# Two-layer diffusion backbone on one core: three of layer 1's modulation products moved to layer 0's router and to the gap between the layers

## The reference, cut to what matters

```python
mod = silu(c) @ w_mod[l] + b_mod[l]          # one row of 6 * 1024 for each group
shift1, scale1, gate1, shift2, scale2, gate2 = split(mod, 6)
y = token_mixing(x * (1 + scale1) + shift1, ...)
x = layer_norm(ALPHA * x + gate1 * y, ...)
y = hier_moe(x * (1 + scale2) + shift2, ...)
x = layer_norm(ALPHA * x + gate2 * y, ...)
```

## Time and profile before

| | us |
|---|---|
| timed executions | 1424.7, 1426.8, 1427.19 |
| median | 1426.8 |
| profiled execution, its own time | 1428.1 |
| profiled execution, span from first to last instruction | 1426.3 |
| layer 1: input projection to router | about 730 to 1155 |
| layer 0: router to first expert | about 445 to 482 |

### The profile page before, as it was taken

The page is one execution under the profiler, slowest core; times in us unless marked ns, Lnnn a source line. Parts: engine busy times, 40 slices in busy tenths (PEclk is TensorE's granted clock), DMA queues, the critical chain, the costliest instruction groups (busy, mean ns, idle before and its releaser), DMA issues. The chain is left out here.

```text
span 1426.3 us, 17205 instructions
## 1 busy us (share of the span) xinstructions
PE 1360.6 (95%) x6802; PEld 745.1 (52%) x6802; DVE 509.1 (36%) x975; ACT 222.4 (16%) x429; POOL 148.8 (10%) x130
## 2 busy tenths in 40 slices
PE   5999999999999999999989999999999999999994
PEld 2665545445445655555537655544554465555552
DVE  1224454432134422322352345452413343232324
ACT  0021220222201111111110213122230111011110
POOL 0002431022100000000001034302120000000000
PEclk9999999999999999999999999999999999999998
DMA  9755545556457399999964635544436729999993
GB/s 380 259 209 196 213 191 181 210 198 244 197 198 315 138 392 370 414 412 413 393 260 157 243 139 182 195 170 189 175 139 265 295 76 395 404 390 396 412 411 138
DMA packets 44345, 376.31 MB, mean 264 GB/s; under 512 B 13050, under 2 KB 17274, under 8 KB 21628
## 3 DMA queue, kind: packets, MB, share of 16 engines
q1 hardware_dynamic: 35856, 372.18, 65.1%
q10 hardware_dynamic: 8428, 3.29, 0.9%
HBM read 371.11 MB, written 4.33 MB: 263 GB/s over the span
## 5 line engine op out<-in xcount | busy, mean ns | idle before, releaser
L943 PE MATMUL psum<-ring,hT 128*128 128x512 f32 x960 | 432.0, 598 | 5.1 <-DVE hT L1398 2.5
L943 PEld LDWEIGHTS psum<-ring,hT 128*128 128x128 f32 x960 | 177.3, 191 | 206.1 <-issue 198.4
L1049 PE MATMUL psum<-ring,tbuf 128*64 128x256 f32 x1920 | 216.0, 380 | 3.6 <-DMA ring<-in_stream 3.6
L1049 PEld LDWEIGHTS psum<-ring,tbuf 128*64 128x64 f32 x1920 | 135.9, 137 | 97.1 <-issue 17.8
L1088 PE MATMUL psum<-ring,tbuf 128*64 128x512 f32 x512 | 116.9, 598 | 3.1 <-ACT tbuf L1332 1.9
L1755 DVE TENSOR_SCALAR tbuf<-tbuf 128x256 f32<-128x256 f32 x32 | 9.4, 295 | 244.5 <-ACT tbuf L1322 244.5
L1609 DVE TENSOR_TENSOR ch<-psum,bias_ring 128x512 f32<-128x512 f32 x56 | 38.7, 691 | 140.3 <-PE psum L943 140.3
L939 PE MATMUL psum<-hT,ring 128*128 128x256 f32 x384 | 85.4, 380 | 0.0
L967 PE MATMUL psum<-ring,tbuf 128*128 128x512 f32 x192 | 82.9, 593 | 0.0
L939 PEld LDWEIGHTS psum<-hT,ring 128*128 128x128 f32 x384 | 72.5, 190 | 13.0 <-issue 3.7
L1913 POOL TENSOR_SCALAR ldata<-ldata 128x512 f32<-128x512 f32 x24 | 46.1, 1922 | 257.3 <-ACT ldata L1284 245.6
(11 more groups left out here) (270 smaller groups left out, 1172.5 us busy)
## 6 DMA issues: line engine op xcount, KB each, us to landing
ring<-in_stream SPq DMA_DIRECT2D x158, 2048.0 KB, 9.7
ch<-in_stream SPq DMA_DIRECT2D x6, 2048.0 KB, 13.0
bias_ring<-in_b_in SPq DMA_DIRECT2D x30, 256.0 KB, 8.0
ldata<-in_ldata SPq DMA_DIRECT2D x2, 2329.0 KB, 19.8
hbuf<-in_ln SPq DMA_DIRECT2D x4, 1024.0 KB, 12.4
hbuf<-in_stream SPq DMA_DIRECT2D x1, 2048.0 KB, 8.7
tbuf<-in_stream SPq DMA_DIRECT2D x1, 2048.0 KB, 11.9
hbuf<-row_mem SPq DMA_DIRECT2D x2, 1024.0 KB, 4.7
```

Of the source, the lines that this page charges most:

```text
L943: mm = pe.matmul(bank(PJ + g), hT[:, k, g * P:(g + 1) * P], w[:, k, :], start=(k == 0), stop=(k == KT - 1))
L1049: mm = pe.matmul(psum[halves_of[hf], UP[j], 0:FE // 2], xgT[:, k, halves_of[i]], w_up[:, k, hf * (FE // 2):(hf + 1) * (FE // 2)], start=(k ...
```

## The change

Layer 1 keeps five modulation slots in its own projection, 7 to 11, after chunks 2, 5, 8, 11 and 14. Slots 4 and 5 are multiplied at layer 0's router in place of `hold_clock` products, both into bank 5, which DVE adds once. Slot 6 is multiplied between the layers into bank 1; ACT copies the bank to `sig`, and POOL adds that to `rows`. Slot 4 is loaded to `tbuf`, slot 5 in two halves to parts of `ch` and `hbuf`, slot 6 to the first `ahead_slot`. Because half of slot 5 lies where the constants of the second normalisation go, SP waits for the two router products ahead of `norm_and_gates`. The `hold_clock` products that remain at the router go to other PSUM areas.

```diff
-              dict(zip([2, 4, 6, 8, 10, 12, 14, 16], [(1, m) for m in range(4, N_MOD)]))]
+              dict(zip([2, 5, 8, 11, 14], [(1, m) for m in range(7, N_MOD)]))]
+ROUTER_MODS, LAYER_MODS = [4, 5], [6]
...
+        mod_half = [chf[:, 0:SLOT // 2], hbuf[:, 0:SLOT // 2]]
...
                 for j in range(AHEAD):
                     sp.dma_start(ahead_slot[j], dram["stream"][l * SLOTS + FIRST_EXPERT_SLOT + j]).then_inc(ahead_loaded[j], 16)
+                if l + 1 < DEPTH:
+                    sp.dma_start(early_slot[1], dram["stream"][stream_slot("mod", l + 1, ROUTER_MODS[0])]).then_inc(router_mod_loaded[0], 16)
                 sp.wait_ge(yt_ready, l * 4 + 4)
+                if l + 1 < DEPTH:
+                    for i in range(2):
+                        sp.dma_start(mod_half[i], dram["stream"][stream_slot("mod", l + 1, ROUTER_MODS[1]), :, i * (SLOT // 2):(i + 1) * (SLOT // 2)])\
+                          .then_inc(router_mod_loaded[1], 16)
+                    sp.wait_ge(router_mods_filled, 1)
                 norm_and_gates(l, 1)
...
                 first_pass()
+                if l + 1 < DEPTH:
+                    for j, m in enumerate(LAYER_MODS):
+                        sp.dma_start(ahead_slot[j], dram["stream"][stream_slot("mod", l + 1, m)]).then_inc(layer_mods_loaded[j], 16)
...
+                def router_mod(m, w, start, stop):
+                    for k in range(KT):
+                        j = k % 4
+                        mm = pe.matmul(psum[MROWS * j:MROWS * (j + 1), 5, :], scZ[:, k, ZC - 2 * m:ZC - 2 * m + MROWS], w[k],
+                                       start=(start and k < 4), stop=(stop and k >= 4))
+                    return mm
...
                         x_turned(l, 0, g)
+                        if g == 1:
+                            pe.wait_ge(layer_mods_copied, 1)
...
                 tokens_back(0)
-                hold_clock(3)
+                if l + 1 < DEPTH:
+                    hold_clock(1)
+                    pe.wait_ge(router_mod_loaded[0], 16)
+                    w = early_slot[1].rearrange("p (k n) -> p k n", k=KT)
+                    router_mod(ROUTER_MODS[0], [w[:, k, :] for k in range(KT)], True, False)
+                else:
+                    hold_clock(3)
                 turn_x(l, 1, 1, 6)
-                hold_clock(2)
+                hold_clock(4, psum[:, 4, W // 2:W])
...
                 tokens_back(1)
-                hold_clock(5)
+                if l + 1 < DEPTH:
+                    pe.wait_ge(router_mod_loaded[1], 32)
+                    w = [half_.rearrange("p (k n) -> p k n", k=KT // 2) for half_ in mod_half]
+                    router_mod(ROUTER_MODS[1], [w[k // 4][:, k % 4, :] for k in range(KT)], False, True).then_inc(router_mods_filled, 1)
+                    hold_clock(3, bank(7))
+                else:
+                    hold_clock(5, bank(7))
...
                 if l + 1 < DEPTH:
-                    hold_clock(3)
+                    for j, m in enumerate(LAYER_MODS):
+                        pe.wait_ge(layer_mods_loaded[j], 16)
+                        mm = mod_products(ahead_slot[j].rearrange("p (k n) -> p k n", k=KT), m, 1, True, True)
+                    mm.then_inc(layer_mods_filled, 1)
+                    hold_clock(2)
...
                         modulate(l + 1, 0, g, 2 + 2 * g)
+                        if g == 0:
+                            act.wait_ge(layer_mods_filled, 1)
+                            act.activation(sig, bank(1), ACT.Copy).then_inc(layer_mods_copied, 1)
...
+                if l + 1 < DEPTH:
+                    dve.wait_ge(router_mods_filled, 1)
+                    dve.wait_ge(rows_added, MOD_ADDS.index((1, ROUTER_MODS)))
+                    tt(rows[:, l + 1, :], rows[:, l + 1, :], bank(5), ALU.add).then_inc(rows_added, 1)
                 dve.wait_ge(ranked, l + 1)
...
+                if l + 1 < DEPTH:
+                    pool.wait_ge(layer_mods_copied, 1)
+                    pool.wait_ge(rows_added, MOD_ADDS.index((1, LAYER_MODS)))
+                    tt(rows[:, l + 1, :], rows[:, l + 1, :], sig, ALU.add).then_inc(rows_added, 1)
```

More of the change, by code:

```diff
@@ L77 @@
 MODS_AFTER = [dict(zip([2, 3, 5, 6, 7, 9, 10, 11, 13, 14, 15, 16], [(0, m) for m in range(4, N_MOD)] + [(1, m) for m in range(4)])),
-              dict(zip([2, 4, 6, 8, 10, 12, 14, 16], [(1, m) for m in range(4, N_MOD)]))]
-MOD_ADDS = [(0, m) for m in EARLY_MOD] + [(l, [m]) for after in MODS_AFTER for l, m in after.values()]
+              dict(zip([2, 5, 8, 11, 14], [(1, m) for m in range(7, N_MOD)]))]
+ROUTER_MODS, LAYER_MODS = [4, 5], [6]
+MOD_ADDS = [(0, m) for m in EARLY_MOD] + [(l, [m]) for l, m in MODS_AFTER[0].values()] \
+    + [(1, ROUTER_MODS), (1, LAYER_MODS)] + [(l, [m]) for l, m in MODS_AFTER[1].values()]
 MROWS = 32
@@ L409, in build @@
         mod_ready = sem("mod_ready")
+        router_mod_loaded = [sem(f"router_mod_loaded{i}") for i in range(len(ROUTER_MODS))]
+        router_mods_filled = sem("router_mods_filled")
+        layer_mods_loaded = [sem(f"layer_mods_loaded{i}") for i in range(len(LAYER_MODS))]
+        layer_mods_filled, layer_mods_copied = sem("layer_mods_filled"), sem("layer_mods_copied")
         rows_summed = sem("rows_summed")
@@ L496, in all_added @@
         def all_added(l):
-            return 2 + sum(len(after) for after in MODS_AFTER[:l + 1])
+            return 2 + len(MODS_AFTER[0]) if l == 0 else len(MOD_ADDS)
         def used(l, i):
@@ L892, in turn_branch, with hold_clock @@
                     mm.then_inc(br_turned, 1)
-                def hold_clock(n):
+                def router_mod(m, w, start, stop):
[4 more added lines that the diff above has]
+                    return mm
+                def hold_clock(n, out_=bank(5)):
                     for _ in range(n):
-                        pe.matmul(bank(5), ident, const[:, 0:W], start=True, stop=True)
+                        pe.matmul(out_, ident, const[:, 0:out_.shape[-1]], start=True, stop=True)
                 def before_first_chunk(q):
@@ L1282, in _ @@
                         act.wait_ge(proj_read, proj(l, c, g))
+                        if (l, c, g) == (1, 12, 0):
+                            act.wait_ge(rows_added, MOD_ADDS.index((1, LAYER_MODS)) + 1)
                         v = ch[:, g, GATE_BUF[c - 12], :]
```

## The result

The changed kernel takes 1418.2 us (median of four runs, 1416.7 to 1420.7), the kernel before 1426.05 beside it: ratio 0.9947, 95% interval 0.9932 to 0.9963, 7.9 us less.

A forecast was written before the change was run, and what follows sets the result against it. PE's own queue was taken to bound the kernel (busy 95% of the span). Projections -5.6, router +0.14 and gap +0.2 gave -5.2 us, from the median 1426.8 to 1421.6 us; range 1419.5 to 1425.2.

The forecast's parts named there:

- 3 x 1.86: Layer 1's projections: net three products leave PE's queue, each holding PE for 1.86 us, 5.6 us in all.
- Later expert slots are issued when PE frees a buffer, as before: Layer 0's experts: loads after the first slots keep their issue rule; no gain or cost was counted.
- Projections: Layer 1's projections: five products out, two in, 5.6 us less; bounds 5.9 with pauses, 1.9 if two products give nothing.
- Rival 1: Layer 1's projections: the time comes back as waits behind chunks 10 and 12, leaving -1.6 us, 1425.2; chance 0.14.
- Router: Layer 0's router: the second product with its fillers takes 4.44 instead of 4.30 us, costing 0.14, up to 0.3.
- The first product is covered: Layer 0's router: slot 4's product ends at 457.94, before DVE's normalised `x` at 458.01, so it costs nothing.
- Loads behind SP's wait: Layer 0's first expert slots land near 478.6, 483.5 and 488.4, margins 3.9, 2.5 and 3.0 us: no cost.
- rivals 2 and 3: Layer 0's first expert loads late: by up to 0.6 us (1422.2 us, chance 0.08), or 9.2 us (1432.3 us, chance 0.05).
- Gap: Between the layers: group 0's turn comes about 1.0 us later, layer 1's first chunk about 0.2; bounds 0 and 1.0.
- ACT's cover: Between the layers: ACT's part of the modulation had 0.8 us to spare before the first chunk, all used up.
- rival 4: Layer 0's router: the change doesn't do what it says, a clock that falls there; near 1427 us, chance 0.03.
- the range's low end: Whole kernel: 5.9 us gained and no costs, 1420.9, less 1.4 for the spread of the runs: 1419.5 us.

The follow-up runs named there:

- e4: The changed kernel unaltered, run again beside the kernel before for more runs and a second profile: 1420.4 us (seven runs, ratio 0.9962).

## Why the prediction missed, point by point

Two steps failed. "3 x 1.86" was too small a price for three products, by some 0.4 us. "Later expert slots are issued when PE frees a buffer, as before" took PE's waits for those slots as a constant; that, as far as the profiles tell, is most of the rest and what put the time outside the range. Another 0.75 us of the distance to the forecast is its base: the kernel before stood at 1426.8 us when the forecast was made and at 1426.05 beside the changed one.

- **Projections: right in kind, 0.45 us short.** Forecast 5.6, bound 5.9; measured 6.06, and 6.02 as the mean of four profiles each. The step that failed is "3 x 1.86". The 1.86 runs from the product's start to that of the work behind it. PE's starts, matched between the two profiles, show two more pieces. Behind chunk 10 the projection ahead of the product starts at 933.40 and the round behind it at 938.78, 5.38 us apart; without the product it is 932.13 and 935.57, 3.44. So 1.94 goes, 0.1 of it ahead of the product. The round behind then takes 1.78 us instead of 1.89 to the next projection, another 0.1:

```profile
933.40 3.60 PE L943 MATMUL psum<-ring,hT 128*128 128x512 f32 x8
```

  In this way each of the five products taken out wins 2.01 to 2.05 us, and each of the two put in costs 2.05. The prediction had the piece ahead, as 0.1 a product, in the bound and not in the sum; it had nothing for the piece behind. Rival 1 is out: no round came late, and PE's waits are still 1.2 and 0.6 us, as in the earlier trace rows (790 to 1110 us):

```profile
PE psum L878 <- issue: 1.2, 1, 1.2
...
PE psum L878 <- ACTq L1294: 0.6, 1, 0.6
```

- **Router: 0.33 against 0.14**, 0.25 net of the 0.08 won behind it. The first product is covered, as said: PE turns `x` at 459.13, 1.06 later than before, and all was 1.07 late. The four narrow fillers take what the two wide ones took (460.06 to 461.97, against 458.99 to 460.91). The second product with its fillers takes 4.54 us instead of 4.30, 0.1 more than forecast, and 0.1 lies ahead of it, where I had nothing: from the second `tokens_back` to the next product it is 1.00 us (463.75 to 464.75), and before it was 0.90 (462.69 to 463.59). DVE's add does fit into the time in which it would wait for PE's ranking:

```profile
468.33 0.69 DVE L1763 TENSOR_TENSOR rows<-rows,psum 128x512 f32<-128x512 f32 x1
470.06 0.19 DVE L1766 SCALAR_TENSOR_TENSOR tbuf<-psum,tbuf 128x32 f32<-128x32 f32 x1 [1.04 <-PE psum L1063]
```

- **Loads behind SP's wait: right.** The first three slots landed at 480.4, 485.1 and 490.0, 4.7 and 4.9 us apart, that is 2048 KB in 4.9 us or 428 GB/s, and PE waited for none of them, so rivals 2 and 3 are out. They came 1.6 to 1.8 us later than forecast, 1.1 of it because all stood 1.07 us later. The Trainium skill, "DMA: Bandwidth & Descriptors", section "Measured", gives 425 GB/s for 16 MB loaded by a core that streams alone, and these landings agree with that. They do not agree with the 358 of the Trainium skill's section "Specifications" on that page.
- **Gap: 0.03 against 0.2.** The turn came 0.86 later (728.59 against 727.05, less the 0.68 by which the last expert product was late), and ACT's cover is used up, as worked out: ACT ends at 731.23 and DVE at 731.25. But neither is what the first chunk waits for. PE goes from its two fillers into the chunk at 731.34 with no idle time; the 0.76 us that it idled there before took up most of the 0.86. The prediction reckoned with ACT's cover and not with PE's fillers. The four profiles of the kernel before have 13.65 to 14.51 us here (above), so this one pair says little of the 0.2. The window from 723 to 735 us has the granted clock at 0.86, 0.88 before, and rival 4's place, 463 to 470, has it at 1.00:

```profile
463.00:470.00 7.00, 7.00 (x47) 3.96 (x46) 4.39 (x24) 1.39 (x4) 0.00 (x0) 1.00 0.29 98
723.00:735.00 12.00, 11.74 (x41) 4.76 (x42) 11.24 (x20) 2.61 (x9) 1.09 (x1) 0.86 0.95 375
```

- **What was left out.** The parts of the first pair sum to 6.02 - 0.33 + 0.08 - 0.03 = 5.7 us (6.1 with the gap's mean of four profiles), and 5.9 were measured over all runs; the first comparison gave 7.9. For its two profiles the table shows where the other 2 us lie: 2.8 won in the experts and 1.07 lost in the start. The medians also hold runs that have no profile; for them it is an inference that the same waits scatter. The step that failed is "Later expert slots are issued when PE frees a buffer, as before", which took PE's waits for them as a constant. They are 2.3 to 6.0 us in a profile, and the kernel before's profile stood at the top of that. The start up to the router scatters as well, by 2.7 us over the eight profiles; why, no run shows. So the range's low end, with 1.4 us for the spread of runs, was too near for a median of four. That the first comparison came out at 7.9 and not nearer to 5.9 was luck. Of the 1.4 us by which the mean waits differ, some 0.6 lie in layer 0, where the four profiles of either kernel don't overlap (1.97 to 2.54 us before, 1.17 to 1.94 after); that may be a lasting gain, by way of the instruction packets' place, but it isn't shown. The rest can't be told from chance by four profiles each.

## What to carry to other kernels

Split the span at marks on the bounding engine and compare the stretches over several executions of both kernels: here the router and the projections repeat to 0.05 us, where single runs of one kernel lie up to 6 us apart (1421.7 to 1428.0 in one batch), so two executions of each say what the change is worth in these stretches better than the medians do. The gap, which ends on a load, scattered by 0.9 us and needs more. Ask first which waits in the profile one predicts from belong to that execution alone: waits for loads in a loop that runs at the pace of DMA do. Price a product that is taken out from the start of the work before it to the end of the work behind it, not from its own start to the next: here 2.0 us against 1.86.

## What the runs showed of the hardware

- A load of 2048 KB ends with sixteen small packets and lands with the last of them. One that lagged by 2.0 us in e4 delayed six slots in a row until the queue ran dry, and such a lag came in some executions of one program and not in others.
- PE's code comes as packets of 16384 bytes among the DMA's (41 in the changed kernel's profile), and 50 of 58 smaller lags of a slot's load started while one was under way.
- PE's branch behind the experts took 3.4 to 3.7 us in eight profiles, in which PE multiplied nothing for 2.2 to 2.6, and up to 5.4 us (4.24 with no product) with a 2048 KB load under way. In each it ended 1.3 to 1.5 us after an instruction packet. The Trainium skill, "Advanced Engine Details and Errata", section "Control Flow Timing", gives about 108 ns for a compare-and-branch; this one took some thirty times that. The Trainium skill, "Advanced Engine Details and Errata", section "ISA Cache", has lines of 16 KB, 256 instructions; the size of the trace's packets agrees, and their count of instructions no run here shows.
